# Two experts at a time: the expert loop of an MoE decoder step regrouped into pairs on TensorE

## The reference

```python
def moe_ffn(h, p):
    t = h.reshape(b * s, d)                                  # 264 tokens x 1024
    scores = jax.nn.sigmoid((t @ p['w_router']).astype(jnp.float32))
    ...                                                      # top 6 of 64 experts per token, weights w
    gte = jnp.einsum('td,edf->tef', t, p['w_gate_e'])        # 64 experts, 1024 -> 256
    upe = jnp.einsum('td,edf->tef', t, p['w_up_e'])
    routed = jnp.einsum('tef,efd->td', jax.nn.silu(gte) * upe * combine[:, :, None], p['w_down_e'])
    shared = (jax.nn.silu(t @ p['w_gate_s']) * (t @ p['w_up_s'])) @ p['w_down_s']
    return (routed + shared).reshape(b, s, d)
```

## Time and profile before

| | us |
|---|---|
| median of 3 runs | 944.06 (943.67 to 945.27) |
| span of the profiled execution | 942.6 |
| median less span (launch and end around it) | 1.46 |
| TensorE busy | 899.4 (95%) |
| VectorE busy | 329.6 (35%) |
| ScalarE busy | 201.5 (21%) |
| moved by all DMA queues | 325.47 MB |

### The profile page before, as it was taken

The page is one execution under the profiler, slowest core; times in us unless marked ns, Lnnn a source line. Parts: engine busy times, 40 slices in busy tenths (PEclk is TensorE's granted clock), DMA queues, the critical chain, the costliest instruction groups (busy, mean ns, idle before and its releaser), DMA issues.

```text
span 942.6 us, 18259 instructions
## 1 busy us (share of the span) xinstructions
PE 899.4 (95%) x7475; PEld 558.1 (59%) x7475; DVE 329.6 (35%) x826; ACT 201.5 (21%) x507; POOL 154.5 (16%) x185
## 2 busy tenths in 40 slices
PE   5999999998899899999899999999999999999997
PEld 3888888876565577647645545444444545455442
DVE  2325570046344698347123222221122222221224
ACT  2000110316122398034111111110111111111102
POOL 0000000031466000101212212121212212112110
PEclk9999999999999899999999999999999999999999
DMA  9966767636699838998999999999999999999992
GB/s 363 390 241 230 299 231 273 264 122 228 202 341 347 325 128 330 404 417 322 326 384 411 425 416 424 418 422 418 424 417 424 416 422 418 423 418 425 417 398 110
DMA packets 61237, 325.47 MB, mean 345 GB/s; under 512 B 16321, under 2 KB 25394, under 8 KB 40610
## 3 DMA queue, kind: packets, MB, share of 16 engines
q1 hardware_dynamic: 47218, 305.53, 80.7%
q0 software_dynamic: 12176, 18.56, 5.9%
q10 hardware_dynamic: 1760, 0.20, 0.2%
HBM read 326.65 MB, written 15.81 MB: 363 GB/s over the span
## 4 chain that ended last, share of the span: by engine, by line
PE 47%; DMA 4%; DVE 1%; ACT 0%; issue 0%
PE bank L2383 23%; PE bank L2323 12%; PE bank L2334 7%; DMA slot_b<-in_w_e 4%; PE bank L2295 3%; PE bank L2417 1%; PE bank L2369 1%; DVE slot_b L2700 0%; DVE slot_b L2708 0%; PE bank L2353 0%; PE bank L2361 0%; DVE hh L2599 0%; ACT sge L2510 0%; ACT slot_b L2527 0%; ACT xt L2501 0%
## 5 line engine op out<-in xcount | busy, mean ns | idle before, releaser
L420 PE MATMUL bank<-h,ring 128*128 128x264 f32 x608 | 138.4, 388 | 0.5 <-PE bank L420 0.3
L420 PEld LDWEIGHTS bank<-h,ring 128*128 128x128 f32 x608 | 114.6, 190 | 21.9 <-issue 2.8
L2510 ACT ACTIVATE sge<-bank 64x256 f32<-64x256 f32 x64 | 24.2, 377 | 392.8 <-PE bank L2383 392.8
L2599 DVE TENSOR_TENSOR hh<-sge,bank 64x256 f32<-64x256 f32 x64 | 27.1, 423 | 227.7 <-ACT sge L2510 227.7
L2383 PE MATMUL bank<-done_out,xt 128*64 128x256 f32 x832 | 95.5, 382 | 0.0
L2383 PE MATMUL bank<-ring,xt 128*64 128x256 f32 x800 | 93.5, 387 | 0.3 <-ACT xt L2501 0.3
L1677 POOL DMA_INDIRECT xg<-tok_rows,tab_g x32 | 32.1, 1004 | 338.5 <-PE bank L2295 328.5
L2556 DVE COPY sq<-bank 128x512 f32<-128x512 f32 x64 | 44.3, 692 | 103.6 <-PE bank L2323 100.4
L2323 PE MATMUL bank<-ring,ht 128*32 128x512 f32 x320 | 76.4, 598 | 0.0
L2383 PEld LDWEIGHTS bank<-done_out,xt 128*64 128x64 f32 x832 | 57.9, 137 | 27.6
L2383 PEld LDWEIGHTS bank<-ring,xt 128*64 128x64 f32 x800 | 56.7, 139 | 27.6 <-issue 0.5
(11 more groups left out here) (487 smaller groups left out, 1247.5 us busy)
## 6 DMA issues: line engine op xcount, KB each, us to landing
done_out<-in_w_e SPq DMA_DIRECT2D x26, 2048.0 KB
ring<-in_w_units SPq DMA_DIRECT2D x25, 2048.0 KB, 11.3
ring<-in_w_e SPq DMA_DIRECT2D x24, 2048.0 KB
slot_b<-in_w_e SPq DMA_DIRECT2D x13, 2048.0 KB
ring<-in_w_e SPq DMA_DIRECT2D x19, 1024.0 KB
slot_b<-in_w_e SPq DMA_DIRECT2D x10, 1024.0 KB
done_out<-in_w_e SPq DMA_DIRECT2D x10, 1024.0 KB
row_of<-in_w_e SPq DMA_DIRECT2D x10, 1024.0 KB
```

The costliest lines, as they stand in the source:

```text
L420: mm = pe.matmul(bank[:, t % NB, 0:T], w[:, j, k, :], h[:, k, :], start=(k == 0), stop=(k == KD - 1))
L2510: act.activation(sg[e % 2][:, :], bank[0:LB, 4, 0:FE], ACT.Silu).then_inc(sg_ready, 1)
L2599: dve.tensor_tensor(hh[e % 2][:, :], sg[e % 2][:, :], bank[LB:2 * LB, 4, 0:FE], ALU.mult).then_inc(hh_ready, 1)
```

## The change

The unit of the loop on TensorE becomes a pair q of experts 2q and 2q+1: gate/up of both (the second into bank 5), both turn halves of the next pair (banks 6 and 7), the inner transposes of both experts at once (the upper half of bank 4), both combines of the pair before, then both down halves of this same pair (banks 6 and 7). `ht` becomes two tiles of 4 blocks for four of 2. Small products that used bank 7 move to bank 5. VectorE does two multiplies, one routing matrix, one copy `ht` of twice the size, and two `half_out`. ScalarE does silu twice and then both `xt` copies. SyncE issues the two down loads ahead of the pair's two gate/up loads, and the first four half loads ahead of the gate/up loads of experts 62 and 63.

```diff
@@ SyncE
                         for e in range(NE):
+                            if e % 2 == 0 and 2 <= e < NE - 8:
+                                for n in (e + 4, e + 5):
+                                    if n != EXTRA:
+                                        load_dn(sp, n)
                             if e + SLOTS < NE:
                                 load_gu(sp, e + SLOTS)
-                            if e % 2 and 3 <= e < NE - 7:
-                                for n in (e + 3, e + 4):
-                                    if n != EXTRA:
-                                        load_dn(sp, n)
-                            if e == NE - 6:
+                            if e == NE - 8:
                                 load_dn_halves(sp, NE - 4)
                             if e == NE - 5:
                                 load_dn_halves(sp, NE - 2)
@@ TensorE
+                        def gate_up(e):
                             pe.wait_ge(gu_in[e % SLOTS], 16 * gu_times(e))
                             pe.wait_ge(xt_ready, e // 2 * 2 + 2 if e else 1)
-                            if e:
-                                pe.wait_ge(hh_ready, e)
+                            if e >= 2:
+                                pe.wait_ge(hh_ready, e - 1)
+                            if e >= 2 and e % 2 == 0:
+                                pe.wait_ge(ht_ready, e // 2)
...
+                        for q in range(NPAIR):
+                            gate_up(2 * q)
...
+                            gate_up(2 * q + 1)
+                            if q + 1 < NPAIR:
+                                for h in range(2):
+                                    turn_half(q + 1, h)
+                            turn_inner(q)
+                            if q:
+                                combine(2 * q - 2)
+                                combine(2 * q - 1)
...
+                            for h in range(2):
+                                down_half(q, h)
...
                         combine(NE - 2)
                         combine(NE - 1)
@@ down_half
-                            pe.wait_ge(ht_ready, 2 * q + 2)
+                            pe.wait_ge(ht_ready, q + 1)
...
+                            if q + 1 < NPAIR:
+                                pe.wait_ge(xt_ready, 2 * q + 3 + h)
+                            else:
+                                pe.wait_ge(y_ready, 2 * q - 1 + h)
@@ ScalarE
-                            if e + 2 < NE:
+                            if e % 2 and e + 2 < NE:
+                                rows_half(e + 1)
                                 rows_half(e + 2)
@@ VectorE
+                        for q in range(NPAIR):
+                            for e in (2 * q, 2 * q + 1):
+                                dve.wait_ge(sg_ready, e + 1)
+                                if q:
+                                    dve.wait_ge(ht_done, q)
+                                dve.tensor_tensor(hh[e % 2][:, :], sg[e % 2][:, :], bank[LB:2 * LB, 4 + e % 2, 0:FE], ALU.mult).then_inc(hh_ready, 1)
+                            if q:
+                                weight_matrix(q - 1)
+                            dve.wait_ge(ht_done, q + 1)
...
+                            half_out(2 * q)
+                            half_out(2 * q + 1)
```

More of the change, by code:

```diff
@@ L2111, in build @@
                 hh = [sb(f"hh{i}", [LB, FE], stack=ph) for i in range(2)]
-                ht = [sb(f"ht{i}", [P, 2, LB], stack=ph) for i in range(4)]
+                ht = [sb(f"ht{i}", [P, 4, LB], stack=ph) for i in range(2)]
                 wmat = [sb(f"wmat{i}", [P, P], stack=ph) for i in range(2)]
@@ L2340, in counts @@
                                 for a in tiles:
-                                    mm = pe.matmul(bank[0:1, 7, (4 + i) * NE:(5 + i) * NE], ones[:, 0:1], chosen[:, a, :],
+                                    mm = pe.matmul(bank[0:1, 5, (4 + i) * NE:(5 + i) * NE], ones[:, 0:1], chosen[:, a, :],
                                                    start=(a == tiles[0]), stop=(a == tiles[-1]))
@@ L2347, in spread_weights @@
                             pe.wait_ge(w6_ready, 1)
-                            pe.matmul(bank[0:TS * TOPK, 7, 2 * P:2 * P + TOPK], spread, w6[:, :], start=True, stop=True).then_inc(spread_done, 1)
+                            pe.matmul(bank[0:TS * TOPK, 5, 2 * P:2 * P + TOPK], spread, w6[:, :], start=True, stop=True).then_inc(spread_done, 1)
                         def sample_rows(n):
@@ L2352, in sample_rows @@
                                 for c in range(4):
-                                    mm = pe.matmul(bank[32 * c:32 * c + TS, 7, (2 + i) * P:(3 + i) * P],
+                                    mm = pe.matmul(bank[32 * c:32 * c + TS, 5, (2 + i) * P:(3 + i) * P],
                                                    (samp[:, 2, 2 * c + i, :], x1_s[:, 2 * c + i, :])[n], ident, start=True, stop=True)
@@ L2360, in shared_rows @@
                                 for c in range(4):
-                                    mm = pe.matmul(bank[32 * c:32 * c + 32, 7, 256:512], hs_s[:, k, :], w_sd[:, k, c * QD:(c + 1) * QD],
+                                    mm = pe.matmul(bank[32 * c:32 * c + 32, 5, 256:512], hs_s[:, k, :], w_sd[:, k, c * QD:(c + 1) * QD],
                                                    start=(k == 0), stop=(k == 1))
@@ L2399, in _, with turn_inner @@
-                            if e == 8:
+                        def turn_inner(q):
+                            pe.wait_ge(hh_ready, 2 * q + 2)
+                            for e in range(2):
+                                for k in range(2):
+                                    at = FE + (2 * e + k) * LB
+                                    mm = pe.transpose(bank[:, 4, at:at + LB], hh[e][:, k * P:(k + 1) * P], eye)
+                            mm.then_inc(ht_done, 1)
+                        for h in range(2):
+                            turn_half(0, h)
@@ L2400, in _ @@
+                        for q in range(NPAIR):
+                            gate_up(2 * q)
+                            if q == 4:
                                 pe.wait_ge(over_ready, 1)
-                            if e == 10:
+                            if q == 5:
                                 pe.wait_ge(wc_ready, 1)
-                            if 12 < e <= 14:
-                                pe.wait_ge(rowt_took, e - 12)
-                            if e == 7:
+                            if q in (7, 8):
+                                pe.wait_ge(rowt_took, q - 6)
+                            if q == SHARED_S_AT // 2 + 1:
+                                pe.wait_ge(shs_took, 1)
+                            gate_up(2 * q + 1)
[6 more added lines that the diff above has]
+                                combine(2 * q - 1)
+                            if q in (SHARED_AT // 2, SHARED_AT // 2 + 1):
+                                shared_down(2 * q - SHARED_AT)
+                                shared_down(2 * q - SHARED_AT + 1)
+                            for h in range(2):
+                                down_half(q, h)
+                            if q == 3:
@@ L2416, in _ @@
-                            for k in range(2):
-                                mm = pe.transpose(bank[:, 7, k * LB:(k + 1) * LB], hh[e % 2][:, k * P:(k + 1) * P], eye)
-                            mm.then_inc(ht_done, 1)
-                            if e == NE // 2:
-                                more = overflow(pe)
-                        down_half(NPAIR - 2, 1, 5)
-                        combine(NE - 4)
-                        down_half(NPAIR - 1, 0, 6)
-                        combine(NE - 3)
@@ L2549, in _, with half_out @@
                     def _(dve):
-                        def half_out(n, b):
+                        def half_out(n):
                             q, h = n // 2, n % 2
```

108 lines of the change are left out of this document (34 added, 74 removed).

## The result

| | before | after |
|---|---|---|
| median, us | 944.32 (941.07 to 950.18, 16 runs) | 948.62 (943.61 to 950.81, 16 runs) |
| profiled execution: time, us | - | 946.46 |
| span of the profiled execution, us | 942.6 | 944.3 |

The ratio after to before is 1.0032, with a 95% interval of 1.0017 to 1.0046: 3.0 us slower, where 0.7 us slower was forecast. The two medians lie 4.3 us apart, at the upper end of that interval; the text goes by the ratios. Two later measurements of the same kernel gave 1.0018 (0.9998 to 1.0037) and 1.0023 (1.0005 to 1.0042), so its place is about 0.25% above before. The forecast of "no change" was wrong: the first median lies outside both ranges of the prediction (up to 946.6 and up to 947.2), and two of the three intervals lie wholly above 1.

A forecast was written before the change was run, and what follows sets the result against it. The DMA queue was taken to decide, with TensorE nearly level: last wait 894.18 plus 10.41 and 28.02 puts combine 62 at 932.61, +0.7 us, so 943.3 us of span and 944.8 of time; 8-in-10 range 942.0 to 947.2.

The forecast's parts named there:

- no change: Whole kernel: +0.7 us, 944.8 us of time, within the 0.2% a measurement can tell; chance 0.56 of staying within.
- A pair takes 13.91 us on TensorE, 0.53 less: TensorE's loop: longer groups of the same work take 13.91 us per pair for 14.44.
- the wait for the inner chain: Inner transposes need silu and multiply, 1.09 us; the turn covers 0.99, so 0.1 shows per pair, all 1.09 in the last.
- The queue decides; waits once per pair from about pair 20: DMA needs 15.69 us per pair, TensorE 13.91; the lead runs out, then TensorE waits for each odd expert's gate/up weights.
- The early gain of 1.7 us: Start of the loop: down places come free sooner, so the queue runs empty less; gain between 0 and 2.8 us, 1.7 taken.
- Gate/up 59 at 894.18, no wait for weights behind it: Last wait for weights: gate/up 59 lands at 895.88 less 1.7 early gain; TensorE then no longer waits for weights.
- Combine 62 starts at 932.61: End of the loop: 894.18 plus 10.41 for the rest of pair 29 and 28.02 for pairs 30 and 31; before 931.89.
- Both `xt` copies and the routing matrix end before the combines do: Within a pair: these copies and the matrix are covered by the combines, so no wait was counted for them.
- Around the span 1.46 us: Outside the profiled span of 942.6 us: 1.46 us more give the median of 944.06; added to the forecast span of 943.3.
- The clock as a rival: TensorE's clock falls to half after the wait for gate/up 59: 1.7 us on top of the forecast, 946.5 us; chance 0.12.

The follow-up runs named there:

- light loads: Down loads from expert 6 on cut to a quarter of their bytes, in both kernels: before 942.07 us (ratio 1.0003), after 925.46 us (ratio 0.9814).
- matrix experiment: Changed kernel with the routing matrix of pair 31 built ahead of the last two copies of down results on VectorE: 945.28 us, 1.0006 of before.
- two loads behind: Changed kernel with pair 31's routing matrix built early and the down loads of experts 58 and 59 behind gate/up 59's load: 943.98 us, 1.0011 of before.
- halves: Changed kernel, pair 31's routing matrix early, down loads 58 and 59 behind gate/up 59's, gate/up 63 loaded in two halves: 941.85 and 942.82 us, 1.0003 and 0.9994 of before.
- order of use: Changed kernel, routing matrix early, gate/up 63 loaded in halves, down loads from expert 28 behind their pair's gate/up load: 941.70 and 942.59 us, 0.9977 and 0.9983 of before.

## Why the prediction was wrong

Its steps, one by one:

- *A pair takes 13.91 us on TensorE, 0.53 less.* Right: 13.90. The turn (1.02), inner transposes (0.33), combines (1.92) and down halves (3.57; 901.06 to 904.63) are within 0.1 us of what was worked out, and the wait for the inner chain shows only in the last pair (0.94 us; 1.09 forecast, with 0.1 in each other pair).
- *The queue decides; waits once per pair from about pair 20.* Right: 17.1 us of waits for 17 saved, though they begin sooner, in pair 17 (gate/up 35, at 707.53). The light loads show it directly, 16.6 us.
- *The early gain of 1.7 us.* Right in mechanism, wrong in its split: the window shows 22 GB/s more than before over 40 us, 2.1 us, but by the order alone 13 GB/s, 1.2 us. The profile of before had its first gate/up at half clock, and the prediction took the clock there to be low after the change too; in none of the three profiles of after was it.
- *Gate/up 59 at 894.18, no wait for weights behind it.* The second half is right. The time is luck: counted from the first gate/up it came 1.4 to 2.4 us sooner than forecast.
- *"Combine 62 starts at 932.61"*: this step failed. It was the sum of TensorE's own work, and held only if nothing else was late at combine 62. The prediction put the wait for the routing matrix at nothing, with "Both `xt` copies and the routing matrix end before the combines do". That holds within a pair; I had then treated the last pair like the others, but its routing matrix is not made inside the loop. TensorE waited 1.16 us for it. It cost 1.05 us against the forecast in the profile, and 1.24 by the matrix experiment.
- *Around the span 1.46 us.* Mis-sized: this term was a median less the span of another execution. In each later execution of any kernel time less span was 2.0 to 2.2 us (946.46 - 944.3 = 2.16). That is 0.7 us in the absolute time and nothing in the ratio.
- *The clock as a rival.* It fell once behind such a wait: the gate/up at 771.32 took 5.36 us, and the granted clock from 768 to 780 us was 0.86. Waits of 1.0 to 1.7 us at ten more places of that execution left gate/up at 3.67, and the two other executions of the kernel show no fall there. The length of the wait does not settle it: the same gate/up stands behind waits of 2.01, 2.02 and 2.03 us in three other profiles (matrix early, two loads behind, halves for the second time) and took 3.67 in each. The rule of the Trainium skill on oscillation ("TensorE: Matmul & The Clock Gate", section "HAM oscillation — how this bites in real kernels") has as its traced case a kernel whose waits for DMA are longer than those of the loops here. The prediction stretched it to every pair, and the trace agrees with that in one row alone. Behind the gate/up at 771.32 the next pair had no wait and the one after 0.61 us for some 1.1 in the other executions, so most of it was absorbed. It did not decide.

So the cause splits as follows. Forecast against before: +0.7 us. With the missed wait it is +1.8 (0.7 + 1.05), which is what the second and third measurement give (1.0018 and 1.0023: +1.7 and +2.2). The distances, with before at full clock, say +1.1 to +2.0. The first measurement gave +3.0 us, its interval reaching down to 1.6; the 1.2 us above are not more than it leaves open. In absolute time the first median is 3.8 us over the 944.8 forecast: 1.05 us are the missed wait, 0.7 the time around the span, and the other 2.1 are how far the profiled execution (946.46) lies below the median of its own measurement (948.62). These 2.1 us stay unexplained; the missed wait alone would not have carried the time out of the range. What was wrong in kind was one instruction's place on an engine that is 35% busy.

## What to carry to other kernels

When a loop is turned from items to groups, go through the first and the last group by itself, and ask of every instruction behind the loop what now stands ahead of it on its queue; an engine with much idle time delays the end all the same if a ready instruction stands behind one that waits. Where two resources are nearly level, a saving on one turns into waits for the other: price it at the last wait and by the work that stands behind it. Then change the order of what the other one delivers so that it matches the order of use, except where an early place keeps the queue from running empty. Take the time around the span from the same execution as the span. And before two profiles are compared, look whether the clock fell in one of them only: here one first gate/up at half clock was as large as the effects to be told apart.

## What the runs showed of the hardware

Most of what single executions differ by goes with TensorE's clock ahead of the expert loop, in code that no kernel here changes. Windows in two profiles, after for the second time, whose execution took 949.1 us:

```profile
200.00:300.00 100.00, 91.94 (x1180) 62.30 (x1184) 51.21 (x114) 34.05 (x100) 51.28 (x64) 0.95 0.78 259
300.00:400.00 100.00, 92.12 (x713) 69.41 (x706) 68.11 (x145) 54.46 (x179) 5.39 (x15) 0.93 0.76 291
```

and the one with gate/up 63 in halves, 939.62 us:

```profile
200.00:300.00 100.00, 92.98 (x1238) 62.84 (x1238) 53.13 (x118) 35.91 (x105) 55.35 (x76) 0.98 0.81 275
300.00:400.00 100.00, 90.97 (x697) 66.98 (x690) 66.19 (x140) 53.38 (x176) 2.43 (x4) 1.00 0.79 308
```

0.95 and 0.93 stand against 0.98 and 1.00, and the first gate/up starts at 461.51 against 453.85. These are nearly the extremes of the fourteen profiles; from the first gate/up to the end of the span the three of after lie within 0.9 us of each other (485.5 to 486.4). Over all executions of all kernels the time falls by 0.56 us for each 0.001 of mean granted clock, by a line fitted within each kernel; it accounts for about half of the scatter (55% of the variance). Set to the same clock by it, the second and third measurement of after lie 1.9 and 1.3 us above before (the first has no clocks of before beside it), the matrix edit 0.4 above, and the order of use 2.6 and 1.6 below, in the same order of kernels as by the ratios. Why the clock falls in one execution and not in the next is open.
